# Moving a transformer block's modulation rows off GpSimd and behind other work

## What is computed

```
mod = silu(c) @ w_ada + b_ada            # 6 * 1024 numbers, one set for the sequence
shift_m, scale_m, gate_m, shift_f, scale_f, gate_f = split(mod, 6)
h = rms_norm(x, norm_mix) * (1 + scale_m) + shift_m
u_ssm, c_q, c_kv, k_rope = split(h @ w_in)
y_ssm  = gelu(s5(u_ssm)); y_ssm = y_ssm * sigmoid(y_ssm @ w_glu + b_glu)
y_attn = latent attention over c_q, c_kv, k_rope (8 heads, causal)
x  = x + gate_m * (concat(rms_norm(y_ssm), rms_norm(y_attn)) @ w_out)
h2 = rms_norm(x, norm_ffn) * (1 + scale_f) + shift_f
x + gate_f * peer_ffn(h2)                # 8 heads x 16 experts out of 16384 per token
```

## Time and profile before

| | us |
|---|---|
| median of 3 runs | 3100.2 (3099.12 to 3102.09) |
| the profiled execution | 3097.78 |
| its span, first to last instruction | 3096.0 |
| DVE busy in the span | 2219.7 (72%) |
| PE busy in the span | 2306.5 (74%) |
| POOL busy in the span | 1331.6 (43%) |

### The profile page before, as it was taken

One profiled execution on the slowest core, in us unless ns is written; L12 is line 12 of the kernel. 1 busy time (PEld: TensorE's weight loads), 2 busy tenths in 40 slices (PEclk: granted clock), 3 DMA queues, 4 the chain that ended last, 5 costly groups with the idle time before them and its releaser, 6 DMA issues.

```text
span 3096.0 us, 38203 instructions
## 1 busy us (share of the span) xinstructions
PE 2306.5 (74%) x13062; PEld 1889.7 (61%) x13062; DVE 2219.7 (72%) x5219; ACT 2038.7 (66%) x3768; POOL 1331.6 (43%) x1177
## 2 busy tenths in 40 slices
PE   7979889878887966767776766776677676666766
PEld 4755568767774655666665665665566665556655
DVE  7887569888875857776777677677666767777644
ACT  4225258888775656777667767766777667766675
POOL 4122134344443544444444445444454444544442
PEclk9989989989887987787767777767776767777766
DMA  6143299999999999999999999999999999999997
GB/s 228 19 182 113 114 370 419 402 363 397 382 403 419 389 419 422 421 421 420 421 420 410 419 422 420 413 416 419 418 415 420 416 422 420 414 421 416 417 421 321
DMA packets 176212, 1159.42 MB, mean 374 GB/s; under 512 B 23568, under 2 KB 25488, under 8 KB 44560
## 3 DMA queue, kind: packets, MB, share of 16 engines
q0 software_dynamic: 147984, 1075.90, 84.3%
q1 hardware_dynamic: 28032, 81.06, 7.2%
HBM read 1146.27 MB, written 9.44 MB: 373 GB/s over the span
## 4 chain that ended last, share of the span: by engine, by line
DMA 32%; DVE 26%; PE 16%; ACT 10%; issue 4%; POOL 1%; POOLq 0%; DVEq 0%; ACTq 0%
DMA pair<-in_experts_dram,idx_g 31%; DVE pair L1933 12%; PE acc_a L1552 5%; ACT pair L1710 4%; PE acc_b L1552 3%; PE pef L1527 2%; ACT L1706 1%; POOL pair L1383 1%; DVE top_i L1861 1%; ACT w L1708 1%; DVE staged L1862 1%; DVE top_i L1864 1%; PE pef L1445 1%; PE acc_b L1475 1%; DVE top_v L1863 1%
## 5 line engine op out<-in xcount | busy, mean ns | idle before, releaser
L1383 POOL DMA_INDIRECT pair<-in_experts_dram,idx_g x1024 | 1227.8, 1199 | 1422.6 <-PE acc_a L1552 796.6
L1933 DVE SCALAR_TENSOR_TENSOR pair<-pair,h 128x1024 f32<-128x1024 f32 x1024 | 1246.1, 1221 | 640.4 <-DMA pair<-in_experts_dram,idx_g 638.9
L1710 ACT ACTIVATE pair<-pair,w 128x1024 f32<-128x1024 f32 x1024 | 1176.5, 1149 | 33.4
L1552 PE MATMUL acc_a<-ident,pair 128*128 128x128 f32 x5120 | 849.3, 327 | 386.4 <-ACT pair L1710 381.0
L1552 PEld LDWEIGHTS acc_a<-ident,pair 128*128 128x128 f32 x5120 | 720.5, 170 | 506.6 <-ACT pair L1710 480.1
L1552 PE MATMUL acc_b<-ident,pair 128*128 128x128 f32 x3072 | 585.2, 357 | 296.8 <-ACT pair L1710 296.6
L1552 PEld LDWEIGHTS acc_b<-ident,pair 128*128 128x128 f32 x3072 | 481.5, 186 | 393.6 <-ACT pair L1710 388.1
L1706 ACT ACTIVATE ga<-a 128x1 f32<-128x1 f32 x1024 | 204.4, 200 | 673.4 <-DVE pair L1933 668.3
L1708 ACT ACTIVATE w<-ga,g 128x1 f32<-128x1 f32 x1024 | 301.6, 295 | 33.2
L1527 PE MATMUL pef<-h2t,wq 128*128 128x128 f32 x1536 | 201.7, 295 | 0.0
L1527 PEld LDWEIGHTS pef<-h2t,wq 128*128 128x128 f32 x1536 | 200.6, 214 | 1.0 <-issue 1.0
(11 more groups left out here) (380 smaller groups left out, 2306.1 us busy)
## 6 DMA issues: line engine op xcount, KB each, us to landing
pair<-in_experts_dram,idx_g POOLq DMA_INDIRECT x1024, 16.2
wrow<-in_w_ada_t_dram SPq DMA_DIRECT2D x11, 1024.0 KB, 5.7
pieces<-in_w_query_t_dram SPq DMA_DIRECT2D x18, 512.0 KB, 8.5
wada<-in_w_ada_t_dram SPq DMA_DIRECT2D x16, 512.0 KB, 8.7
wq<-in_w_query_t_dram SPq DMA_DIRECT2D x4, 2048.0 KB, 31.3
out_dram<-h SPq DMA_DIRECT2D x8, 512.0 KB, 8.7
wout_b<-in_w_out_dram SPq DMA_DIRECT2D x1, 4096.0 KB, 34.8
pool_rows<-in_w_ada_t_dram SPq DMA_DIRECT2D x1, 3072.0 KB, 12.0
```

Of the source, the lines that this page charges most:

```text
L1383: p.indirect_dma_start(pair[n % R], None, A["experts"], bass.IndirectOffsetOnAxis(ap=idx[:, t % (2 * PH), k:k + 1], axis=0)).then_inc(pair ...
L1552: last = t.matmul(accs[ACC[i]][:, k * P:(k + 1) * P], pair[n % R][:, D + k * P:D + (k + 1) * P], S.ident[:], is_transpose=True, start=n % ...
L1710: s_.activation(pair[n % R][:, D:], pair[n % R][:, D:], ACT.Copy, scale=w[:, n % NA:n % NA + 1]).then_inc(scaled, 1)
L1933: v.scalar_tensor_tensor(down, down, 1.0, h2[:, n // P, :], ALU.mult, ALU.mult, accum_out=a[:, n % NA:n % NA + 1]).then_inc(dotted, 1)
```

## The change

POOL no longer does any elementwise work on rows or squares. In phase AB, DVE adds the squared blocks (`add_square`), one behind each of the columns from the third on. In phase C, DVE weighs rows 16 to 43 (28 instead of 26) through four buffers instead of three, the load `pool_rows` and what POOL and ACT did with it are gone, and each gate product stands ahead of the rows of its b instead of behind them. The sums of squares of b are one block later on PE. The last four rows (44 to 47) are loaded by SP and weighed by DVE in the attention phase, with a copy of silu(c) that ACT makes in phase D; the bias addition that DVE did at the start of phase D for six of them is now done for four of them in the attention phase.

```
@@ phase_ab, gpsimd
-            for k in range(1, KD):
-                pool.wait_ge(sq_ready, k + 1)
-                if k >= 2:
-                    pool.wait_ge(sq_added, k - 1)
-                nc.gpsimd.tensor_tensor(sqx[:, 0], sqx[:, 0], sqx[:, k], ALU.add).then_inc(sq_added, 1)
@@ phase_ab, vector
+            def add_square(k):
+                dve.wait_ge(sq_ready, k + 1)
+                if k >= 2:
+                    dve.wait_ge(sq_added, k - 1)
+                v.tensor_tensor(sqx[:, 0], sqx[:, 0], sqx[:, k], ALU.add).then_inc(sq_added, 1)
+
...
                 v.scalar_tensor_tensor(S.a_m[:, k:k + 1], S.mod[:, b:b + 1], 1.0, S.vec[:, V_NM + k:V_NM + k + 1], ALU.add, ALU.mult).then_inc(am_ready, 1)
-            for n in range(KD, 2 * KD):
+                if k >= 2:
+                    add_square(k - 1)
+            weigh_row(KD)
+            add_square(KD - 1)
+            for n in range(KD + 1, 2 * KD):
                 weigh_row(n)
@@ phase_c
-    wrow = [place(nc, f"wrow{n}", [P, 2, D], 50 + 8 * n) for n in range(3)]
-    FIRST_ROW, ROWS, POOL_ROWS = GATE_M, 26, 6
-    pool_rows = place(nc, "pool_rows", [P, POOL_ROWS, D], 103)
+    wrow = [place(nc, f"wrow{n}", [P, 2, D], kb) for n, kb in enumerate((50, 58, 66, 103))]
+    FIRST_ROW, ROWS = GATE_M, 28
+    NW = len(wrow)
@@ phase_c, sync
             sp.wait_ge(x_ready, 8)
-            for n in range(1, ROWS // 2 - 1):
-                if n >= 3:
-                    sp.wait_ge(row_used, 2 * n - 2)
-                if n == 3:
-                    sp.dma_start(pool_rows[:], w[:, FIRST_ROW + ROWS:FIRST_ROW + ROWS + POOL_ROWS, :]).then_inc(S.rows_ssm_keys_in, 16)
-                sp.dma_start(wrow[(n - 1) % 3][:], w[:, FIRST_ROW + 2 * n + 2:FIRST_ROW + 2 * n + 4, :]).then_inc(row_in[n % 3], 16)
+            for n in range(ROWS // 2 - 2):
+                if n >= NW:
+                    sp.wait_ge(row_used, 4 + 2 * (n - NW + 1))
+                sp.dma_start(wrow[n % NW][:], w[:, FIRST_ROW + 4 + 2 * n:FIRST_ROW + 6 + 2 * n, :]).then_inc(row_in[n % NW], 16)
@@ phase_c, tensor
-            square_sums(0)
             for b in range(2, 8):
                 glu(b, (0, 1, 2, 3))
-                square_sums(b - 1)
+                square_sums(b - 2)
+            square_sums(6)
             square_sums(7)
@@ phase_c, vector
             weigh_rows(0, 8)
             steps_out(7)
+            weigh_rows(8, 11)
             for b in range(8):
-                weigh_rows(8 + 2 * b + min(b, 2), 10 + 2 * b + min(b + 1, 2))
                 dve.wait_ge(g_out, b + 1)
...
                                 gate[:, b % 2].rearrange("p (i n) -> p i n", n=P), ALU.mult).then_inc(g_mul, 1)
+                weigh_rows(11 + 2 * b + min(b, 1), 13 + 2 * b + min(b + 1, 1))
@@ phase_c, gpsimd
-            pool.wait_ge(S.rows_ssm_keys_in, 16)
-            for r in range(POOL_ROWS):
-                p.tensor_tensor(pool_rows[:, r], pool_rows[:, r], S.silu_c[:], ALU.mult).then_inc(row_mul, 1)
@@ phase_c, scalar
-                if b >= 2:
-                    sum_row(b - 2)
@@ phase_d
             s.activation(root_first[:], S.eps[:], ACT.Sqrt)
+            s.activation(S.silu_late[:], S.silu_c[:], ACT.Copy)
...
-            own.mark(v.tensor_tensor(S.mod[:, later], S.mod[:, later], S.vec[:, V_BA + GATE_F + 2:V_BA + GATE_F + KD], ALU.add))
@@ phase_ef, sync, behind the load of x2_a[:, 1]
+            sp.wait_ge(S.yst_out, 16)
+            for r in range(S.LATE):
+                sp.dma_start(late_rows[r][:], w[LATE_AT + r]).then_inc(S.yst_out, 16)
@@ phase_ef, vector
+            def weigh_late(first, end):
+                dve.wait_ge(S.yst_out, 16 * (1 + S.LATE))
+                for r in range(first, end):
+                    own.mark(v.scalar_tensor_tensor(late_rows[r][:], late_rows[r][:], 1.0, S.silu_late[:], ALU.mult, ALU.mult,
+                                                    accum_out=S.mod[:, LATE_AT + r:LATE_AT + r + 1]))
...
             at_back(0)
+            weigh_late(0, 2)
             head_step(H)
             make_base(0)
             head_step(H + 1)
+            weigh_late(2, 4)
+            own.wait()
+            own.step(v.tensor_tensor(S.mod[:, LATE_AT:], S.mod[:, LATE_AT:], S.vec[:, V_BA + LATE_AT:V_BA + 6 * KD], ALU.add))
             make_x2(0)
```

More of the change, by code:

```diff
@@ L668, in phase_c @@
         sq_ready, sq_summed = sem("c_sq"), sem("c_sqs")
-        row_in, row_used, row_mul = [sem(f"c_row_in{n}") for n in range(3)], sem("c_row_used"), sem("c_row_mul")
+        row_in, row_used = [sem(f"c_row_in{n}") for n in range(NW)], sem("c_row_used")
         block = ctx.enter_context(nc.Block())
@@ L835, in weigh_rows @@
                 for r in range(first, end):
[L836 to L838 removed]
+                    n, b = r // 2 - 2, FIRST_ROW + r
+                    if r < 4:
+                        dve.wait_ge(S.heads_in, 64)
+                    else:
+                        dve.wait_ge(row_in[n % NW], 16 * (n // NW + 1))
+                    wb = wfour[:, r] if r < 4 else wrow[n % NW][:, r % 2]
                     v.scalar_tensor_tensor(wb, wb, 1.0, S.silu_c[:], ALU.mult, ALU.mult, accum_out=S.mod[:, b:b + 1]).then_inc(row_used, 1)
@@ L857, in _ @@
         def _(pool):
[L858 to L863 removed]
+            nc.gpsimd.memset(ones[:], 1.0).then_inc(ones_made, 1)
         @block.scalar
@@ L888, in steps_out @@
                              turn_bank(b)[:].rearrange("p (i c) -> p i c", i=4), ACT.Copy).then_inc(tr_out_a, 1)
-            def sum_row(r):
-                b = FIRST_ROW + ROWS + r
-                act.wait_ge(row_mul, r + 1)
-                s.activation(pool_rows[:, r], pool_rows[:, r], ACT.Copy, accum_out=S.mod[:, b:b + 1])
             for b in range(4):
```

22 lines of the change are left out of this document (10 added, 12 removed).

## The result

| | before | after |
|---|---|---|
| median, us | 3099.66 (3094.31 to 3102.09, 4 runs) | 3075.6 (3072.94 to 3078.33, 4 runs) |
| ratio of the times | | 0.9924, 95% interval 0.9911 to 0.9936 |
| the profiled execution, us | 3097.78 | 3072.94 |
| its span, us | 3096.0 | 3071.0 |

What follows compares the result with a forecast made beforehand. The loop was taken as bound by its DMA fetches, passing on front gains unchanged; in the front, POOL's work stalled DVE and PE waited. 18.3 + 2.8 + 0 = 21.1 us off the median 3100.2 gives 3079; range 3076 to 3082, with rivals 3073 to 3086.

Steps and rivals of the forecast that it cites:

- Cause: In the gate and phase AB: an elementwise instruction on POOL holds DVE up by about 2.1 us, once for each.
- Rival 7: Long DVE instructions come from something else than POOL, so DVE's added work is stretched too: 3149 us, chance 0.01.
- Phase C: The gate: PE sets the pace at 4.33 us a block, last copy at 241.4 instead of 259.7; gain 18.3 us.
- Rivals 1 and 6: 1: gate row loads at 3.8 us a pair, 3082, chance 0.06; 6: late rows starve the gate, slower, chance 0.02.
- Phase AB: DVE's unstalled additions let the tenth row finish earlier, so the sixteenth row's load and PE's work come 2.8 us earlier.
- rival 2: Phase AB: POOL's issue of `win_s` is held until DVE's row run ends, landing late; 3082.6 us, chance 0.04.
- Phase D: The removed bias addition and ACT's copy of silu(c) stand beside PE's first multiplications: 0 us.
- The attention phase: The four late rows cost DVE 4.9 us but fall into its waits of 3.40 and 3.08 us: 0 us.
- Rival 3: Attention phase: the late rows are exposed, by 4.9 us; time 3084 us, chance 0.03.
- The loop: The 1024 slots go at the pace of their fetches, 2690 us, so earlier gains reach the end unchanged.
- Rival 5: The loop takes the gain back: its fetches lose at a crossing with weight loads; 3100 us, no change, chance 0.02.
- rival 4: More gained: no slow clock in phase AB or early phase D, cheaper loop start, 3 us or more; under 3076, chance 0.05.

Runs made afterwards that it cites:

- the repetition: The kernel after itself, unchanged, measured and profiled again on one chip beside a version with two further edits: 3076.6 us (5 runs), ratio 0.9932.
- the run with the rows ahead: Kernel after with three rows ahead of each of the first four gate products, two ahead of the others, none behind the last: 3071.77 us, ratio 0.9917.

## Why the prediction was right

It was right in its cause and in its sum: 3075.6 us for a forecast of 3079, inside 3073 to 3086, though 0.4 us below the forecast's own range of 3076 to 3082. The repetition, 3076.6 us, is in it. Up to the loop's first slot the profiled execution gained 20.9 us (19.3 in the repetition) for the 21.1 forecast, but that closeness is in part luck: phase AB brought 1.8 us more than its term, and phase D took 2.2 that the sum had put at nothing. By its steps:

- **Cause.** GpSimd's elementwise instructions stretch VectorE's, once each by about 2.1 us: shown both ways, by taking them out (3.2 and 3.4 us became 1.22) and by putting six back. Rival 7 is out.
- **Phase C**, forecast 18.3, measured 18.6 in the profiled execution and in its repetition. PE set the pace at 4.33 us a block; the product behind the last block, the two rows and the copy came as worked out; the pairs arrived 2.6 us apart (waits of 0.44 and 0.18 us at 195 and 198, none between gate products). Rivals 1 and 6 are out.
- **Phase AB**, forecast 2.8, measured 4.6, 3.3 in the repetition, and 3.6 with this part alone. The step to the tenth row was exact. Two sizes were off. The sixteenth row's load landed in 7.0 us and not in 8.1, and in all eleven traces with the additions on DVE it took less than 8.1 (6.2 to 7.7); the prediction had taken its time over unchanged. With it PE's idle time ahead of L351 shrank, to 0.45 us, where the prediction had it grow from 2.5 to 3.1. And no slow clock followed in the first profile: that was luck, since the ten others have it. In these eleven traces phase C begins 3.3 to 5.8 us earlier than before, so the term of 2.8 was too small in each.
- **`win_s`**, rival 2: POOL issued it in 1.10 us at 39.35, amid DVE's rows. Out. The prediction took its page too widely here: the box that it draws on in the Trainium skill (SBUF — State Buffer, two separate sides) speaks of VectorE in its two-port modes, and not of every instruction with two inputs in SBUF, so it gave this rival no ground. In all fourteen traces the issue took 1.09 or 1.10 us.
- **Phase D**, forecast 0, measured 2.2 us of loss (1.5 in the repetition). This is the term that I mis-sized. The prediction saw that the two rows at the end are exposed by 1.0 us (0.8 by the run with the rows ahead) and stopped there; it did not ask what the longer gap does to PE's clock. 1.2 us of the 2.2 are in PE's first groups (2.13 + 1.27 us for the second group and the one behind it, 1.19 + 1.02 before). Where the rest of it lies is not shown; with the rows ahead all but 0.2 us of the loss is gone. Over the eight traces with these two rows the loss is 0.7 to 2.3 us. ACT's copy of silu(c), 1.04 us at 238.61, was beside PE's work.
- **The attention phase**, forecast 0, measured 0.1 for the stretch that holds the late rows (13.29 us for 13.18), and 0.1 over all in the profiled execution; in the repetition 1.1. The kernel before without GpSimd's products, which has no late rows, was 1.0 us over the kernel before in the same stretch, so the 1.1 is within the spread. Rival 3 is out.
- **The loop**, forecast unchanged, 4.2 us shorter in the profiled execution. Other kernels with the front of before took 2679.4 (GpSimd's products left out) and 2681.5 us (phase AB alone) from the first to the last slot, those with the front of after 2679.4 to 2686.5. The length is not tied to the front, and its spread over these executions, 7 us, is as large as that of the runs of one kernel. The repetition's 2679.9 us fits both what I had expected (2679 to 2686) and the rival (within 1 us of 2679.4), so it alone decides nothing. Why one execution's loop is longer than another's stays open. Rival 5 is out.

Phase C and phase AB carried the gain. The first measurement is below 3076 us, which is where rival 4 (more is gained) had put the time, but of its three reasons only the missing slow clock in phase AB was there, and by luck: the slow clock at the start of phase D became longer, and the way to the first slot was no shorter. What else set that execution below the forecast was the loop's 4.2 us. The extra over the forecast's 21.1 us (2.5 in the first measurement, nothing in the repetition) is within the spread of the runs.

## What to carry to other kernels

Before moving an elementwise job to GpSimd because it is idle, look at what VectorE does meanwhile. All the VectorE instructions that were stretched here have two inputs in SBUF; beside such, each of GpSimd's additions or multiplications of 128x1024 fp32 cost VectorE about 2.1 us, more than the 1.15 us that the same work takes on VectorE itself. Work that must go somewhere goes into a wait whose size the timeline shows, and not behind the last instruction that another engine waits for: two rows there cost 0.8 us in the open and 0.7 to 2.3 more in the next phase. Measure a moved instruction between two near landmarks of the same trace; over the whole kernel the spread of the main loop hides it.

## What I had not expected of the hardware

- GpSimd's fills, which only write, left VectorE alone entirely: ten of them in 18.57 us, and the rows beside them took 1.22 us.
- The cost to VectorE does not go by the length of VectorE's own instruction: 2.1 us for a row of 1.22, for a product of 0.69 and for an addition of 128x1 (2.19 instead of 0.16).
- A gap of PE that grew from 0.72 to 1.55 us made the first two groups of phase D take 5.7 instead of 4.7 us at the slow clock behind it (granted clock 0.52 from 236 to 240, which is the level of 1.2 GHz for nearly all of it); with the gap filled to 0.30 us they took 3.5.
